# The SSM's table of chunk rotations moves from VectorE to GpSimd

## What is computed

```
mag = jnp.exp(a_re * dt)
lb_re = mag * jnp.cos(a_im * dt)
lb_im = mag * jnp.sin(a_im * dt)
bu_re = jnp.einsum('blgc,gpc->blgp', uf, bb_re)
_, _, xr, xi = lax.associative_scan(_complex_affine_combine, (ar, ai, bu_re, bu_im), axis=1)
y = (einsum(c_re, xr) - einsum(c_im, xi) + d_skip * uf)
out = g * jax.nn.sigmoid(g @ w_glu + b_glu)        # g = gelu(y)
```

## Time and profile before

| | |
|---|---|
| median of 3 runs | 1402.06 us (1400.21 to 1404.23) |
| profiled execution, span from first to last instruction | 1400.8 us |
| PE busy | 1377.8 us, 98% |
| ACT, DVE, POOL busy | 835.7, 685.5, 201.9 us |
| mean granted TensorE clock | 0.997 |

### The profile page before, as it was taken

One profiled execution on the slowest core, in us unless ns is written; L12 is line 12 of the kernel. 1 busy time (PEld: TensorE's weight loads), 2 busy tenths in 40 slices (PEclk: granted clock), 3 DMA queues, 4 the chain that ended last, 5 costly groups with the idle time before them and its releaser, 6 DMA issues.

```text
span 1400.8 us, 18420 instructions
## 1 busy us (share of the span) xinstructions
PE 1377.8 (98%) x6674; PEld 1116.7 (80%) x6674; DVE 685.5 (49%) x1319; ACT 835.7 (60%) x1213; POOL 201.9 (14%) x236
## 2 busy tenths in 40 slices
PE   7999999999999999999999999999999999999998
PEld 4888877777788888888888877777797888888887
DVE  6993478888644455454144154645264301213223
ACT  7556677777655665655365477655666654535442
POOL 1111100101011111111111111110111111111111
PEclk9999999999999999999999999999999999999999
DMA  9996976666589888888888996754767898888973
GB/s 297 221 182 172 223 172 156 137 159 142 133 211 213 195 188 198 186 191 205 194 190 188 211 238 148 177 136 112 160 155 166 194 208 184 207 189 188 201 163 85
DMA packets 82693, 254.76 MB, mean 182 GB/s; under 512 B 16816, under 2 KB 20016, under 8 KB 82608
## 3 DMA queue, kind: packets, MB, share of 16 engines
q0 software_dynamic: 32400, 117.98, 46.8%
q1 hardware_dynamic: 48768, 132.50, 31.2%
q10 hardware_dynamic: 1440, 3.15, 0.6%
HBM read 128.03 MB, written 3.41 MB: 94 GB/s over the span
## 4 chain that ended last, share of the span: by engine, by line
PE 92%; DVE 4%; ACT 2%; DMA 1%; issue 1%; DVEq 0%; ACTq 0%
PE pg L581 27%; PE pg L582 27%; PE pg L583 27%; PE ps L753 2%; PE py L829 1%; PE ps L1011 1%; PE ps L761 1%; PE ps L1019 1%; DMA act_lo<-w_raw 1%; DMA w_lo<-w_raw 1%; DVE pairs L1707 1%; PE py L1029 1%; DVE acc L1710 1%; PE px L654 0%; DVE acc L1707 0%
## 5 line engine op out<-in xcount | busy, mean ns | idle before, releaser
L581 PE MATMUL pg<-x_hi,w_hi 128*128 128x512 f32 x1072 | 423.7, 395 | 2.4 <-ACT rel L1652 2.4
L583 PE MATMUL pg<-x_hi,w_lo 128*128 128x512 f32 x1072 | 418.1, 390 | 0.0
L582 PE MATMUL pg<-x_lo,w_hi 128*128 128x512 f32 x1072 | 418.0, 390 | 0.0
L545 POOL DMA_DIRECT2D w_lo<-w_raw x221 | 190.5, 862 | 1152.3 <-ACT w_lo L1143 1080.6
L1142 ACT ACTIVATE w_hi<-w_raw 128x1024 fp32r<-128x1024 f32 x216 | 227.0, 1051 | 101.5 <-PE pg L583 99.8
L581 PEld LDWEIGHTS pg<-x_hi,w_hi 128*128 128x128 f32 x1072 | 201.5, 188 | 56.4 <-issue 12.1
L583 PEld LDWEIGHTS pg<-x_hi,w_lo 128*128 128x128 f32 x1072 | 201.7, 188 | 42.6
L582 PEld LDWEIGHTS pg<-x_lo,w_hi 128*128 128x128 f32 x1072 | 201.8, 188 | 41.6 <-issue 1.0
L1143 ACT ACTIVATE w_lo<-w_raw 128x1024 fp32r<-128x1024 f32 x216 | 225.9, 1046 | 0.0
L581 PE MATMUL pg<-act_hi,w_hi 128*128 128x512 f32 x424 | 165.1, 389 | 0.8 <-DMA w_lo<-w_raw 0.8
L582 PE MATMUL pg<-act_lo,w_hi 128*128 128x512 f32 x424 | 165.0, 389 | 0.0
(11 more groups left out here) (433 smaller groups left out, 1820.6 us busy)
## 6 DMA issues: line engine op xcount, KB each, us to landing
w_raw<-weights SPq DMA_DIRECT2D x226, 512.0 KB, 4.7
w_lo<-w_raw POOLq DMA_DIRECT2D x221, 512.0 KB, 5.7
kq_rot<-kq_raw SPq DMA_DIRECT2D x64, 64.0 KB, 2.2
hid<-x SPq DMA_DIRECT2D x4, 512.0 KB, 5.5
hid<-x ACTq DMA_DIRECT2D x8, 256.0 KB, 5.4
act_lo<-w_raw POOLq DMA_DIRECT2D x4, 512.0 KB, 8.2
out<-hid SPq DMA_DIRECT2D x16, 128.0 KB, 1.9
u_dram<-hid SPq DMA_DIRECT2D x4, 256.0 KB, 5.4
```

The lines of the kernel that those rows point to most:

```text
L545: pool.dma_start(low_of(u), w_raw[:, s], accum_op=ALU.add).then_inc(lo_in[s], 16)
L581: pe.matmul(bank[:], wh, xh(k), start=n == 0, stop=False)
L582: pe.matmul(bank[:], wh, xl(k), start=False, stop=False)
L583: last = pe.matmul(bank[:], wl, xh(k), start=False, stop=n == len(ks) - 1)
```

## The change

POOL gets the whole table. It waits until DVE's last coefficient is there (L1809 now signals `lane_dve`, and POOL waits for its third count), doubles the angle three times, waits until PE has read the scratch's former content (`bt`), and then fills the table in six rounds. Each round is followed by one of the transfers `lo(5)` to `lo(10)`. An instruction given to `step` is followed on POOL by a wait for its completion. DVE waits for `turns_made` before it rotates the chunk inputs. DVE's scratch for the output tables moves from `y5` to `gates[:, 0:3]`, the repeatedly doubled angles lie in other rows of `lane`, and the skip term stands behind `mag_t`.

```diff
@@ gpsimd
-            for v in range(1, 11):
+            turned = 0
+            def step(ins):
+                nonlocal turned
+                turned += 1
+                ins.then_inc(turn_step, 1)
+                pool.wait_ge(turn_step, turned)
+            def by(out_, a, b, op=ALU.mult):
+                return pool.tensor_tensor(out_, a, b, op)
+            def square_of(c, n, qc, qn):
+                c, n, qc, qn, t = (lane[:, i] for i in (c, n, qc, qn, L_N))
+                by(qc, c, c)
+                by(t, n, n)
+                step(by(qn, c, n))
+                by(qc, qc, t, ALU.subtract)
+                step(by(qn, qn, qn, ALU.add))
+            def doubled(k, pc, pn):
+                n = 1 << k
...
+                by(new_c, old_c, at_n(pc))
+                by(t0, old_s, at_n(pn))
+                by(new_s, old_s, at_n(pc))
+                step(by(t1, old_c, at_n(pn)))
+                by(new_c, new_c, t0, ALU.subtract)
+                step(by(new_s, new_s, t1, ALU.add))
+            pairs_of = [(L_R, L_TH), (L_C2, L_S2), (L_C4, L_S4)]
+            for v in range(1, 5):
                 lo(v, v % RING)
+            pool.wait_ge(lane_dve, 3)
+            square_of(L_COS, L_SIN, L_C2, L_S2)
+            square_of(L_C2, L_S2, L_C4, L_S4)
+            square_of(L_C4, L_S4, *pairs_of[0])
+            ps_ready(pool, ("bt", 1))
+            pool.memset(turn_t[:, 0, :, 0:1], 1.0)
+            step(pool.memset(turn_t[:, 1, :, 0:1], 0.0))
+            for k in range(6):
+                doubled(k, *pairs_of[k % 3])
+                if k < 5:
+                    square_of(*pairs_of[k % 3], *pairs_of[(k + 1) % 3])
+                lo(5 + k, (5 + k) % RING)
+            pool.wait_ge(turn_step, turned)
+            pool.sem_inc(turns_made, 1)
@@ vector
-            link(tt_(L(L_CI), L(L_T1), L(L_T3)))
+            put(tt_(L(L_CI), L(L_T1), L(L_T3)), lane_dve)
...
-                g_t = y5[:].rearrange("p a t -> p (a t)")[:, 0:LANE_T // 2 * (STEP + 1) * GRP]\
+                g_t = gates[:, 0:3, :].rearrange("p a t -> p (a t)")[:, 0:LANE_T // 2 * (STEP + 1) * GRP]\
...
-            square_of(L_COS, L_SIN, L_C2, L_S2)
-            square_of(L_C2, L_S2, L_C4, L_S4)
-            square_of(L_C4, L_S4, L_T1, L_T2)
-            dve.memset(turn_t[:, 0, :, 0:1], 1.0)
-            link(dve.memset(turn_t[:, 1, :, 0:1], 0.0))
-            for k in range(6):
...
+            link(dve.tensor_reduce(m16[:], ident.rearrange("p (j c) -> p c j", c=GRP), AX.X, ALU.add))
...
+            px_read(dve, "kt")
+            put(tt_(kt[:, :, 0:GRP], kt[:, :, 0:GRP], skip[:], ALU.add), kt_made)
...
+            dve.wait_ge(turns_made, 1)
             ps_ready(dve, ("e", 1))
```

More of the change, by code:

```diff
@@ L392, in build @@
         swapped = [sem("swapped_k"), sem("swapped_q")]
+        turn_step, turns_made = sem("turn_step"), sem("turns_made")
         ones_made, lo_first, hi_second = sem("ones_made"), sem("lo_first"), sem("hi_second")
@@ new lines, in doubled, with at_n @@
+            def doubled(k, pc, pn):
+                n = 1 << k
+                def at_n(i):
+                    return lane[:, i, :].rearrange("p (t o) -> p t o", o=1).broadcast_to([P, LANE_T, n])
+                old_c, old_s = turn_t[:, 0, :, 0:n], turn_t[:, 1, :, 0:n]
+                new_c, new_s = turn_t[:, 0, :, n:2 * n], turn_t[:, 1, :, n:2 * n]
+                t0 = gates[:, 4, 0:LANE_T * n].rearrange("p (t n) -> p t n", n=n)
+                t1 = gates[:, 5, 0:LANE_T * n].rearrange("p (t n) -> p t n", n=n)
+                by(new_c, old_c, at_n(pc))
[4 more added lines that the diff above has]
+                step(by(new_s, new_s, t1, ALU.add))
@@ L1817, in times @@
                 return tt_(dst, dst, t0, op)
[L1819 to L1824, removed]
             p_re, p_im = pw[:, 0], pw[:, 1]
@@ L1896, in _ @@
                     put(last, g_made)
-            square_of(L_COS, L_SIN, L_C2, L_S2)
-            square_of(L_C2, L_S2, L_C4, L_S4)
-            square_of(L_C4, L_S4, L_T1, L_T2)
-            pc, pn = L_T1, L_T2
-            spare = [(L_C2, L_S2), (L_C4, L_S4)]
-            dve.memset(turn_t[:, 0, :, 0:1], 1.0)
-            link(dve.memset(turn_t[:, 1, :, 0:1], 0.0))
-            for k in range(6):
[L1905 to L1928, removed]
             link(tt_(L(L_M8), L(L_MAG), L(L_MAG)))
@@ L1933, in _ @@
             link(dve.memset(mag_t[:, :, 0:1], 0.0))
+            link(dve.tensor_reduce(m16[:], ident.rearrange("p (j c) -> p c j", c=GRP), AX.X, ALU.add))
+            link(tt_(skip[:], m16[:].rearrange("p (o c) -> p o c", o=1).broadcast_to([P, SSM_T, GRP]),
+                     pars("ssm_d").rearrange("p (s o) -> p s o", o=1).broadcast_to([P, SSM_T, GRP])))
+            px_read(dve, "kt")
+            put(tt_(kt[:, :, 0:GRP], kt[:, :, 0:GRP], skip[:], ALU.add), kt_made)
             def lanes(bank):
```

## The result

The changed kernel takes 1424.91 us (median of four runs, 1424.19 to 1426.92), the kernel before 1402.26 (four runs, 1400.21 to 1404.23): a ratio of 1.0165, interval 1.0153 to 1.0177. It is slower by 22.7 us. The forecast was 1432, range 1401 to 1441.

What follows compares the result with a forecast made beforehand. The prediction took PE's queue to bound the kernel: three stops for late weights (14.6, 7.5, 4.0 us) and 3.4 us of lower clock, together 29.5, added to 1402.1 gave 1432 us, range 1401 to 1441.

Steps and rivals of the forecast that it cites:

- What bounds, and what is removed: PE, busy 98% of the span, sets the time; taking the table off DVE is worth 0.
- The lock: From 33.7 to 70.47 us each reading POOL instruction waits out a two-input DVE instruction; chance 0.66, 1432 us.
- The sum: PE's three stops for late weights plus slower clock, 14.6 + 7.5 + 4.0 + 3.4 = 29.5 us.
- landing: Time from a weight transfer's issue on POOL to its arrival: the shortest seen, 5.9 us, was taken.
- first stop: PE waits from 47.4 us for unit 5's weights, `lo(5)`, which land at 62.0: 14.6 us.
- second stop: PE ends unit 5 at 67.4 us and waits for `lo(6)`, landed at 74.9: 7.5 us.
- third stop: PE ends unit 6 at 82.2 us and waits for `lo(7)`, landed at 86.2: 4.0 us.
- clock: PE runs at about half clock after a long idle: 1.7 us each for two stops, 3.4 us.
- The price of POOL's instructions: Undisturbed POOL tensor_tensors: 0.14 us for 16 columns up to 1.35 for 512, together 24 us for the table.
- (a): Rival: no lock between two readers, `lo(5)` in time, nothing on PE moves; 1402 us, chance 0.24.
- (b): Rival: no lock, but POOL's short instructions are dear; at 0.3 us each PE stops 3.1 us, 1407; chance 0.07.
- (c): Rival: faster, through a wait of PE on DVE not shown in this execution; at most 1400.2 us, chance 0.03.

Runs made afterwards that it cites:

- experiment 1: The changed kernel with each of POOL's 76 tensor_tensors replaced by a memset of the same output, so POOL reads nothing there: 1401.22 us.
- experiment 4: The kernel before, with 48 reading tensor_tensors of 16 columns, output unused, added on POOL ahead of `lo(5)`, `lo(6)` and `lo(7)`: 1423.45 us.
- experiment 7: The changed kernel with DVE's eighteen input and output table instructions replaced by reductions that read one operand and take as long: 1402.32 us.
- experiment 6: The kernel before, with eight reading tensor_tensors of 512 columns, output unused, added to POOL's queue behind `lo(9)`: 1409.17 us.

## Why the prediction was right

**What bounds, and what is removed**: right. PE still is the chain, and without its table DVE gives nothing back (experiment 1: 1401.22).

**The lock**: right, and shown from three sides (experiments 1, 4 and 7). The row that the forecast leaned on, a TENSOR_SCALAR beside a memset, is of another pair: in experiment 1 memsets beside tensor_tensors aren't held. It pointed the right way without being the same case, so as a ground for the lock it was in part luck. Its own pair shows again in experiment 1: beside POOL's memset of `toep` (68.83 to 72.36 us) DVE's COPY at 70.70, with one input, takes 2.19 us instead of the 0.69 of the kernel before. So a POOL instruction that reads nothing can still hold a copy or a TENSOR_SCALAR of DVE. The Trainium skill (SBUF — State Buffer, § Who interferes with whom) says that the two contend if DVE's instruction has two SBUF inputs and GpSimd's reads SBUF, but not if GpSimd's only writes, nor if DVE's has one input and runs outside its two-port modes; the runs agree with all three, at 1424.91, 1401.22 and 1402.32 us. Whether the held COPY and TENSOR_SCALAR ran in such a mode no run shows. That the time fell into the range says little: 1401 to 1441 was made wide enough to hold the rival without a lock too. The timelines and experiments 1, 4 and 7 are what decides.

**The sum**, term by term (us; landing is from the issue on POOL to SP's next load, which waits for it, at 58.53 and 74.92):

| step | forecast | measured |
|---|---|---|
| `lo(5)` leaves / landing | 56.1 / 5.9 | 53.94 / 4.6 |
| first stop | 14.6 | 11.2 |
| `lo(6)` leaves / landing | 69.0 / 5.9 | 70.09 / 4.8 |
| second stop | 7.5 | 9.0 |
| `lo(7)` leaves | 80.3 | 74.48 |
| third stop | 4.0 | 0 |
| clock | 3.4 | 3.9 |
| DVE's output tables end | about 77 | 71.11 |
| sum | 29.5 | 24.1 |

The mechanism was right and the size 5.4 us too large, 4.0 of it the third stop. **The mis-sized term is what a short POOL instruction costs DVE.** The forecast added POOL's own time to each turn and let DVE's chain end 7 us late; the chain was 0.64 us late. So the first 26 instructions took less (`lo(5)` left 2.2 us earlier), and above all POOL was free from 71.1 us on, not from 77. `lo(7)` then left 5.8 us earlier, and the third stop of 4.0 us doesn't exist. The second error is the landing, 4.6 instead of the shortest 5.9 of the rows. The DMA engines were busy for a share of 0.60 from 53.94 to 58.53 us, against 0.84 to 1.09 in the windows of before; that this is the reason wasn't tested. `lo(6)` went the other way, 1.1 us later: by then DVE had only long instructions left, so all eleven holds were of 1.36 us where the forecast had five of 0.42 among them. These three errors cancel, which is luck: PE begins unit 6 when `lo(6)` has landed, at 74.95 us, and the forecast had 74.9. The remaining 1.3 us are the clock. It was charged at 1.7 us a stop and cost 1.8 and 2.1, but the forecast added the 1.7 us behind the first stop to a sum that already ran to the landing of `lo(6)`: a slower unit 5 only shortens the wait for it. On top of the two waits up to unit 6 (14.6 + 7.5 = 22.1 in the forecast; 11.2 + 1.8 + 9.0 = 22.0 measured) comes only what is lost behind the second, 2.1 us.

**The price of POOL's instructions** was under-read for 16 columns (0.14 forecast, 0.19 from start to start in experiment 7) and over-read for long ones (1.35 for 512 columns, 1.01 measured). Without the lock that is no matter: in experiment 7 `lo(5)` leaves at 40.84 instead of the 39.2 forecast, and PE doesn't wait for it (the 0.8 us at 108.3 are for a later unit).

**The rivals.** (a), no lock, is what experiments 1 and 7 give, at its 1402. (b), dear short instructions without a lock, falls with experiment 7. (c), faster, had no wait to live on. What the forecast named as covered stayed covered: the table at 93.0 us, `toep` and the chunk transfers made PE wait nowhere.

## What to carry to other kernels

Before work is moved to GpSimd, ask which instructions of VectorE run beside it, not how long it takes alone: next to two-input VectorE instructions each of its short reads lasts as long as one of those (2.3 us instead of 0.19 here). And ask what is queued behind it: here it was not the table that came too late but weight transfers issued on the same engine, and moving them ahead only moved the loss to the table (1411). Where such work must go there, put it where VectorE is idle or has one-input instructions like the reductions of experiment 7, and keep transfers that the bottleneck waits for on another queue (which wasn't tried here).

## What was not expected of the hardware

- The lock takes turns, but its cost is lopsided by length: POOL's instructions of 16 and 32 columns cost DVE 0.64 us in all, its 512 column ones about 1 us each (experiment 6).
- In experiment 7 a DVE instruction with two inputs, 0.42 us long elsewhere, took 3.20, from 54.57 to 57.77: it ended 0.3 us after a run of four POOL instructions of 256 columns without a wait between them (54.82 to 57.48), and PE waited 1.1 us at `kernels` for the output tables that stand behind it. I read this as one hold over the whole run; it happened once. Short instructions without waits do take turns one for one (37.85 to 44.75 us in the changed kernel), so longer ones in a row seem able to shut DVE out for the whole row. Which length decides wasn't tried.
- A copy, with one input on POOL, is held as well, but less: 1418.42 us against 1424.91. The cause is open.
